# A two-block transformer kernel: the first units of six following stages computed in two token halves

## The chip, the cores and the metric

The kernel runs on one core of one Trainium2 chip. A core has TensorE (matmul, PE), VectorE (DVE), ScalarE (ACT), GpSimd (POOL) and SyncE, which here only issues loads. TensorE multiplies out of SBUF into PSUM, eight banks of 128 partitions x 512 fp32. Each engine runs its own instruction list; semaphores order them. The metric is device time in microseconds (us) of one execution, lower is better.

## The reference

Input x is 1 x 512 tokens x 1024. Two blocks of two layers each follow one another, in fp32:

```python
for i in range(2):                               # first block, post-norm
    mix = sconv_ssd_mixer(x, ...) if i == 0 else fox_mixer(x, ...)
    x = layer_norm(ALPHA * x + mix, ln_mix_g[i], ln_mix_b[i])
    x = layer_norm(ALPHA * x + conv_ffn(x, ...), ln_ffn_g[i], ln_ffn_b[i])
for i in range(2):                               # second block, gated pre-norm
    sh1, sc1, g1, sh2, sc2, g2 = split(silu(c) @ ada_w[i] + ada_b[i])
    h = rmsnorm(x, norm1_g[i]) * (1 + sc1) + sh1
    x = x + g1 * (gqa_attention(h, ...) if i == 0 else chunked_gmlp(h, ...))
    h = rmsnorm(x, norm2_g[i]) * (1 + sc2) + sh2
    x = x + g2 * (square(relu(h @ mlp_w_in[i])) @ mlp_w_out[i])
```

Each stage needs its input whole in the channel direction: the normalisation takes the mean over all 1024 channels of a token, and each product sums over them.

## The kernel before

**Products.** To keep fp32 accuracy at the speed of the one-pass type fp32r, each operand is split into a high part (its fp32r rounding) and a low part (the rest), and each product is three matmuls: high x high, high x low, low x high. Weights come in *units* of 128 x 1024, 444 in all, through a ring of four slots: SyncE loads `raw`, ScalarE copies it to `whi`, GpSimd subtracts to `wlo` (L558). The products of a 1024-channel input take 24 matmuls of 512 columns per unit.

**Stages.** There are stages of two forms. In the "f" form (`pe_f`: up0, fqk, up1, mu0, mu1) a unit gives 128 output channels for all 512 tokens: the weights stand in the array, the activations `xhi`, `xlo` (channel block k of 8 on the partitions, tokens along the columns) stream through. In the "t" form (`pe_t_unit`) tokens stand in the array. The projections back to 1024 channels (out0, dn0, fo, dn1, o, md0, go, md1; `pe_t_jit`) are of the t form in two column halves, with token tile t of four in PSUM bank t (first half) or 4 + t (second half). Their last two units are ordered by tile in `pe_t_tail`, so that tile 0 is complete first and tile 3 last.

**A boundary.** Between a projection and the next stage lie the residual and the norm. `q` numbers it: 1 is out0 to up0, 2 dn0 to fqk, 3 fo to up1, 4 dn1 to qkv, 5 o to mu0, 6 md0 to gv, 7 go to mu1. For each token tile, VectorE adds the residual (`dve_ln_tile`, or `dve_gated_tile` in the second block), takes the moments, ScalarE takes the root, VectorE the reciprocal and writes `nrm`, in column halves of 512 (the first holds channel blocks 0 to 3). TensorE transposes `nrm` in blocks of 128 x 128 into PSUM banks 0 to 3 (L1897): blocks k = 0 to 3 of each tile as it comes (`pe_xt_tile`), k = 4 to 7 later (`pe_xt_late`), since they use the same four banks. ScalarE applies the norm's gain and shift per channel on the way from PSUM to a two-slot buffer `xf` (`act_xt`, L646), VectorE splits `xf` into `xhi` (a cast, L1217) and `xlo` (a subtract, L1219) (`dve_xt`). Then the first three units of the next stage run k by k, nine matmuls for each k, with one late block's transposes between (`pe_f`, L1987 to L1997).

**Fillers.** `pe_busy` issues transposes of the identity into an unused bank (L1902). `KEEP_BUSY = (0, 18, 0, 16)` puts 18 after tile 1's transposes and 16 after tile 3's in `pe_t_tail`.

**Residual pass.** In boundaries 1 to 3 the residual itself is replaced by the norm's output, `xres = nrm * g + b`, in eight whole-tile operations that `dve_resid` places between the splits (L1491, L1495), beginning after k = 3.

**Order.** All of it is written out by hand, engine by engine. ScalarE copies the next stage's third unit during the tail (`act_next_whi(name, 2)`), its fourth after `act_xt`. In boundary 2 it also loads `wf_raw`, the weights of the forget gate (L1136), ahead of `act_xt` and copies it behind (L1139).

## Time and profile before

| | us |
|---|---|
| median of 3 runs | 2811.45 (2811.03 to 2812.35) |
| the profiled execution, whole | 2811.43 |
| its span, first to last instruction | 2809.5 |
| TensorE busy | 2783.7 (99%) |
| VectorE busy | 1303.3 (46%) |
| GpSimd busy | 1140.6 (41%) |
| ScalarE busy | 1081.2 (38%) |

The page gives busy time by engine; a busy TensorE can also be busy with fillers. Matmuls overlap: a duration of 0.39 us is from the first column in to the last result out, while the next one starts 0.23 us after it. The step from start to start is what a matmul costs in a row. The mean granted clock was 0.998 of full speed.

### The profile page before, as it was taken

To read this page: it belongs to the slowest core of one execution; us is meant where nothing else is said; L and a number is where in the kernel's file an instruction comes from. 1 tells how busy PE (TensorE), PEld (TensorE's weight loads), DVE (VectorE), ACT (ScalarE), POOL (GpSimd) and SP (SyncE) were. 2 spreads that over 40 slices of the span, in tenths; PEclk is the share of its full clock that TensorE was granted. 3 is DMA by queue.
4 is the path that set the end of the run, shared out by engine and by line. 5 is a ranking of instruction groups with operands and counts; after the bars stand their busy time and mean duration, and the time that the engine had idled before them with its cause. 6 is when DMAs were issued, how large, how long until landed. Compare 5 with 4: busy or idle time off the path is not lost.

```text
span 2809.5 us, 37915 instructions
## 1 busy us (share of the span) xinstructions
PE 2783.7 (99%) x13890; PEld 2287.7 (81%) x13890; DVE 1303.3 (46%) x1516; ACT 1081.2 (38%) x1574; POOL 1140.6 (41%) x472
## 2 busy tenths in 40 slices
...
GB/s 160 90 69 74 90 103 267 239 140 88 99 88 95 9 76 232 244 169 102 97 73 45 2 74 106 97 105 98 86 135 94 90 78 103 90 92 96 104 98 75
DMA packets 319812, 299.95 MB, mean 107 GB/s; under 512 B 16268, under 2 KB 251224, under 8 KB 319576
## 3 DMA queue, kind: packets, MB, share of 16 engines
...
## 4 chain that ended last, share of the span: by engine, by line
PE 46%; issue 36%; POOL 16%; DVE 1%; ACT 0%; POOLq 0%; DVEq 0%; ACTq 0%
POOL wlo L558 16%; PE ps L2034 8%; PE ps L2035 8%; PE ps L2036 8%; PE ps L1892 6%; PE ps L1894 6%; PE ps L1893 6%; PE ps L2319 1%; PE ps L2255 1%; PE ps L2284 1%; PE ps L2394 1%; PE ps L2065 0%; PE ps L2067 0%; PE ps L2066 0%; PE ps L1897 0%
## 5 line engine op out<-in xcount | busy, mean ns | idle before, releaser
L558 POOL TENSOR_TENSOR wlo<-raw,whi 128x1024 fp32r<-128x1024 f32 x444 | 1115.3, 2515 | 1630.6 <-ACT whi L616 1630.3
L1892 PE MATMUL ps<-xhi,whi 128*128 128x512 f32 x1824 | 718.0, 394 | 0.3
L1894 PE MATMUL ps<-xhi,wlo 128*128 128x512 f32 x1824 | 710.3, 389 | 0.0
L1893 PE MATMUL ps<-xlo,whi 128*128 128x512 f32 x1824 | 709.9, 389 | 0.0
L616 ACT ACTIVATE whi<-raw 128x1024 fp32r<-128x1024 f32 x444 | 466.3, 1052 | 288.9 <-PE ps L2036 167.8
L2034 PE MATMUL ps<-whi,ahi 128*128 128x512 f32 x1184 | 461.4, 390 | 0.7 <-DVE alo L1396 0.7
L2036 PE MATMUL ps<-whi,alo 128*128 128x512 f32 x1184 | 460.7, 389 | 0.0
L2035 PE MATMUL ps<-wlo,ahi 128*128 128x512 f32 x1184 | 460.6, 389 | 0.0
L1892 PEld LDWEIGHTS ps<-xhi,whi 128*128 128x128 f32 x1824 | 342.5, 188 | 73.1 <-issue 3.2
L1894 PEld LDWEIGHTS ps<-xhi,wlo 128*128 128x128 f32 x1824 | 342.3, 188 | 71.7
L1893 PEld LDWEIGHTS ps<-xlo,whi 128*128 128x128 f32 x1824 | 342.6, 188 | 71.0 <-issue 1.4
L2034 PEld LDWEIGHTS ps<-whi,ahi 128*128 128x128 f32 x1184 | 222.2, 188 | 47.6 <-DVE alo L1396 0.8
L2035 PEld LDWEIGHTS ps<-wlo,ahi 128*128 128x128 f32 x1184 | 222.3, 188 | 46.0
L2036 PEld LDWEIGHTS ps<-whi,alo 128*128 128x128 f32 x1184 | 222.2, 188 | 46.0
L1396 DVE TENSOR_TENSOR alo<-hid_mlp,ahi 128x1024 fp32r<-128x1024 f32 x60 | 76.4, 1273 | 242.1 <-ACT ahi L795 242.1
L1739 DVE SCALAR_TENSOR_TENSOR hid_mlp<-ps,relu 128x512 f32 (+1 forms) x64 | 44.3, 692 | 281.4 <-ACT relu L1033 281.4
L2034 PE MATMUL ps<-whi,xhi 128*128 128x512 f32 x416 | 163.1, 392 | 0.9 <-POOL wlo L558 0.7
L2036 PE MATMUL ps<-whi,xlo 128*128 128x512 f32 x416 | 162.0, 389 | 0.0
L2035 PE MATMUL ps<-wlo,xhi 128*128 128x512 f32 x416 | 161.9, 389 | 0.0
L1541 DVE SCALAR_TENSOR_TENSOR acc<-adaraw,ccol,acc 128x1536 f32<-128x1536 f32 x56 | 154.3, 2793 | 2.4 <-DMA adaraw<-in_ada_w 2.1
L795 ACT ACTIVATE ahi<-hid_mlp 128x1024 fp32r (+1 forms) x60 | 63.7, 1062 | 205.2 <-PE ps L2036 205.2
L1033 ACT ACTIVATE relu<-ps 128x512 f32<-128x512 f32 x64 | 38.3, 599 | 229.3 <-PE ps L1894 229.3
...
## 6 DMA issues: line engine op xcount, KB each, us to landing
...
```

What stands on the lines that cost most here:

```text
L558: pool.tensor_tensor(wlo[:, j], raw[:, j], whi[:, j].bitcast(F32), ALU.subtract).then_inc(w_lo, 1)
L616: act.activation(whi[:, s], raw[:, s], ACT.Copy).then_inc(w_hi, 1)
L795: act.activation(ahi[:, (m0 + j) % 2], x, ACT.Copy).then_inc(a_hi, 1)
L1396: dve.tensor_tensor(alo[:, s], x, ahi[:, s].bitcast(F32), ALU.subtract).then_inc(a_lo, 1)
L1541: dve.scalar_tensor_tensor(x, adaraw[s][:], ccol[:, bass.ds(i, 1)], x, ALU.mult, ALU.add).then_inc(ada_acc, 1)
L1739: dve.scalar_tensor_tensor(hid_mlp[:, bass.ds(e, 1)], ps[:, bank_f(j):bank_f(j) + 1], 0.0, relu[:, j % 2:j % 2 + 1], ALU.max, ALU.mult).th ...
L1892: pe.matmul(out, lh, rh, start=start, stop=False)
L1893: pe.matmul(out, lh, rl, start=False, stop=False)
L1894: return pe.matmul(out, ll, rh, start=False, stop=stop)
L2034: pe.matmul(out, lh[:, k, c], wh[:, k], start=st, stop=False, skip_group_check=True)
L2035: pe.matmul(out, lh[:, k, c], wl[:, k], start=False, stop=False, skip_group_check=True)
L2036: ins = pe.matmul(out, ll[:, k, c], wh[:, k], start=False, stop=False, skip_group_check=True)
```

## The change

At the six boundaries 1, 2, 3, 5, 6 and 7 (`PARTED`) the blocks k = 0 to 3 go through in two parts of 256 tokens: part 0 is tiles 0 and 1, part 1 tiles 2 and 3. TensorE transposes part 0 inside the tail of the projection and part 1 among the products of the next stage. ScalarE applies gain and shift to a half block in place in PSUM, VectorE splits it straight from PSUM. The products of k = 0 to 3 of the first three units run for 256 columns at a time in the f form; gv, of the t form, runs its first two units by pairs of tiles. Blocks 4 to 7 go on as before, but all four are transposed in a row after part 1. The fillers at these boundaries go. The residual pass begins ahead of k = 4. Semaphore counts become the tables `XT0` and `EV0`. Two scratch tiles lay in the room of `xhi`'s first blocks: `gate` moves up by 8 KB, and the squares of the RMS norm, of which only the sums are used, are written to `nrm`. In the diff, `product(e, k, c)` is the three matmuls of unit e and block k on columns c. Its core:

```diff
+PARTED = (1, 2, 3, 5, 6, 7)
+PART = (slice(0, 256), slice(256, 512))
...
+    def act_xt_part(act, q, scale, bias, h):
+        c = PART[h]
+        for k in range(4):
+            act.wait_ge(xt_tp, XT0[q] + 4 * h + k + 1)
+            act.activation(ps[:, k, c], ps[:, k, c], ACT.Identity, scale=scale(k), bias=bias(k)).then_inc(xt_ev, 1)
...
     def act_ln_tail(act, r, name, g_ap, b_ap, scale, bias):
         act_next_whi(act, name, 1)
         act_sqrt_table(act, r)
+        act_ln_std(act, r, 0)
+        act_ln_std(act, r, 1)
+        act_xt_part(act, r + 1, scale, bias, 0)
+        act_ln_std(act, r, 2)
+        act_next_whi(act, name, 2)
+        act_ln_std(act, r, 3)
         load_gb(act, gb, g_ap, b_ap)
+        act_xt_part(act, r + 1, scale, bias, 1)
+        act_xt(act, r + 1, scale, bias, 4)
...
@@ act_rms_tail @@
         for t in range(NT):
-            if t == 2 and early:
-                act_next_whi(act, name, 2)
+            if t == 2:
+                if early:
+                    act_next_whi(act, name, 2)
+                act_xt_part(act, r + 1, norm_scale(s), norm_shift(s), 0)
...
+    def dve_xt_part(dve, q, h):
+        c = PART[h]
+        for k in range(4):
+            dve.wait_ge(xt_ev, EV0[q] + 4 * h + k + 1)
+            dve.tensor_copy(xhi[:, k, c], ps[:, k, c]).then_inc(xt_hi, 1)
+            dve.wait_ge(xt_hi, XT0[q] + 4 * h + k + 1)
+            dve.tensor_tensor(xlo[:, k, c], ps[:, k, c], xhi[:, k, c].bitcast(F32), ALU.subtract).then_inc(xt_lo, 1)
...
@@ dve_ln_tail @@
+        for h in range(2):
+            dve_ln_moments(dve, r, name, h and 3)
+            if not h:
+                dve_ln_moments(dve, r, name, 1)
+            for t in (2 * h, 2 * h + 1):
+                dve_ln_inverse(dve, r, t)
+                norm(t, 0)
+            if not h:
+                dve_ln_moments(dve, r, name, 2)
+            dve_xt_part(dve, r + 1, h)
         for t in range(NT):
             norm(t, 1)
+        dve_xt(dve, r + 1, resid=r, k0=4)
...
@@ dve_rms_tail @@
+        tile(0)
+        tile(1)
+        for t in range(2):
+            inverse(t)
+            norm(t, 0)
+        tile(2)
+        dve_xt_part(dve, 5 + s, 0)
+        tile(3)
+        for t in range(2, 4):
+            inverse(t)
+            norm(t, 0)
+        dve_xt_part(dve, 5 + s, 1)
+        for t in range(NT):
             norm(t, 1)
+        dve_xt(dve, 5 + s, k0=4)
...
@@ pe_f @@
-            for k in range(KD):
-                pe.wait_ge(xt_lo, KD * q + k + 1)
-                for e in range(3):
...
-                if k < 4:
-                    pe_xt_late(pe, q, k + 4)
+            def product(e, k, c, stop=False):
...
+            for h in range(2):
+                for k in range(4):
+                    pe.wait_ge(xt_lo, XT0[q] + 4 * h + k + 1)
+                    for e in range(2):
+                        if not h and k == 0:
+                            pe.wait_ge(w_lo, S + e + 1)
+                            pe.wait_ge(res_add, 8 * q - 3 + e)
+                        product(e, k, PART[h])
+                if h:
+                    for k in range(4, KD):
+                        pe_xt_late(pe, q, k)
+                for k in range(4):
+                    if not h and k == 0:
+                        pe.wait_ge(w_lo, S + 3)
+                        pe.wait_ge(res_add, 8 * q - 1)
+                    if not h and k == 3:
+                        pe_xt_part(pe, q, 1)
+                    product(2, k, PART[h])
+            for k in range(4, KD):
+                pe.wait_ge(xt_lo, XT0[q] + 4 + k + 1)
+                for e in range(3):
+                    ins = product(e, k, slice(0, T), k == KD - 1)
...
+            pe.wait_ge(res_add, 8 * q)
...
@@ pe_t_tail @@
-            if q and q != 4 and t == 2 and i:
-                pe_xt_tile(pe, q, 0)
-        if q:
-            for t in range(0 if q == 4 else 1, NT):
+            if q in PARTED and (t, i) == ((2, 1) if q < 4 else (3, 0)):
+                pe_xt_part(pe, q, 0)
+        if q == 4:
+            for t in range(NT):
...
@@ pe_gm @@
+        unit(0, 0, 1, blocks=XT0[6], tiles=(0, 1), done=False)
+        unit(0, 1, 1, blocks=XT0[6] + 2, tiles=(0, 1), done=False, mid=lambda: pe_xt_part(pe, 6, 1))
         pe.wait_ge(res_add, 48)
+        unit(0, 0, 1, blocks=XT0[6] + 4, tiles=(2, 3))
+        for k in range(4, KD):
+            pe_xt_late(pe, 6, k)
+        unit(0, 1, 1, blocks=XT0[6] + 6, tiles=(2, 3))
```

How it moves instructions, at boundary 1, from the projection's tail to the fourth unit of up0. ScalarE before, from the third and fourth root on (`std` is the root, `xf` the affine, `whi` a weight unit):

```order
L616 ACTIVATE whi<-raw 128x1024 [waits unit_done,raw_in2]
L836 ACTIVATE std<-mv,eps_ln 128x1 [waits aggr_done] x2
L831 DMA gb<-in_ln_mix_g 128x1024
L832 DMA gb<-in_ln_mix_b 128x1024
L646 ACTIVATE xf<-ps,tab 128x512 [waits xt_tp] x2
L646 ACTIVATE xf<-ps,tab 128x512 [waits xt_lo,xt_tp] x6
L853 UNCONDITIONAL_BRANCH
L616 ACT_TABLE_LOAD [waits unit_done]
L616 ACTIVATE whi<-raw 128x1024 [waits raw_in3]
```

ScalarE after, from the first two roots on:

```order
L856 ACTIVATE std<-mv,eps_ln 128x1 [waits aggr_done] x2
L657 ACTIVATE ps<-ps,tab 128x256 [waits xt_tp] x4
L856 ACTIVATE std<-mv,eps_ln 128x1 [waits aggr_done]
L622 ACTIVATE whi<-raw 128x1024 [waits unit_done,raw_in2]
L856 ACTIVATE std<-mv,eps_ln 128x1 [waits aggr_done]
L851 DMA gb<-in_ln_mix_g 128x1024
L852 DMA gb<-in_ln_mix_b 128x1024
L657 ACTIVATE ps<-ps,tab 128x256 [waits xt_tp] x4
L666 ACTIVATE xf<-ps,tab 128x512 [waits xt_lo,xt_tp] x4
L877 UNCONDITIONAL_BRANCH
L622 ACT_TABLE_LOAD [waits unit_done]
L622 ACTIVATE whi<-raw 128x1024 [waits raw_in3]
```

Four half affines now stand between the roots of tiles 1 and 2, four behind the loads of gain and shift, and four whole ones are left.

VectorE before, from tile 0's reciprocal to tile 2's norm (`xres` the residual, `stats` and `mv` the moments):

```order
L1441 RECIPROCAL rstd<-std 128x1 [waits std_done]
L1448 TENSOR_SCALAR nrm<-xres,mv,rstd 128x512 [waits rstd_done]
L1420 SCALAR_TENSOR_TENSOR xres<-xres,ps 128x512 [waits tile_done]
L1422 BN_STATS stats<-xres 128x6 [waits res_add]
L1436 BN_AGGR mv<-stats 128x2 [waits stat_done]
L1441 RECIPROCAL rstd<-std 128x1 [waits std_done]
L1448 TENSOR_SCALAR nrm<-xres,mv,rstd 128x512 [waits rstd_done]
L1448 TENSOR_SCALAR nrm<-xres,mv,rstd 128x512
```

VectorE after, from tile 0's reciprocal to the first half split:

```order
L1479 RECIPROCAL rstd<-std 128x1 [waits std_done]
L1486 TENSOR_SCALAR nrm<-xres,mv,rstd 128x512 [waits rstd_done]
L1479 RECIPROCAL rstd<-std 128x1 [waits std_done]
L1486 TENSOR_SCALAR nrm<-xres,mv,rstd 128x512 [waits rstd_done]
L1458 SCALAR_TENSOR_TENSOR xres<-xres,ps 128x512 [waits tile_done]
L1460 BN_STATS stats<-xres 128x6 [waits res_add]
L1474 BN_AGGR mv<-stats 128x2 [waits stat_done]
L1244 CAST xhi<-ps 128x256 [waits xt_ev]
L1246 TENSOR_TENSOR xlo<-ps,xhi 128x256 [waits xt_hi]
```

Tile 1's reciprocal and norm moved ahead of tile 2's residual, the second-half norm of tile 0 is gone from here, and the splits of part 0 follow tile 2's moments.

VectorE after, from the last half split of part 1 to k = 6:

```order
L1244 CAST xhi<-ps 128x256 [waits xt_ev]
L1246 TENSOR_TENSOR xlo<-ps,xhi 128x256 [waits xt_hi]
L1486 TENSOR_SCALAR nrm<-xres,mv,rstd 128x512 x4
L1531 TENSOR_TENSOR xres<-nrm,gb 128x1024 [waits nrm_done,gb_in]
L1531 TENSOR_TENSOR xres<-nrm,gb 128x1024
L1255 CAST xhi<-xf 128x512 [waits xt_ev]
L1257 TENSOR_TENSOR xlo<-xf,xhi 128x512 [waits xt_hi]
L1535 TENSOR_TENSOR xres<-xres,gb 128x1024 [waits res_mul]
L1255 CAST xhi<-xf 128x512 [waits xt_ev]
L1257 TENSOR_TENSOR xlo<-xf,xhi 128x512 [waits xt_hi]
L1531 TENSOR_TENSOR xres<-nrm,gb 128x1024
L1255 CAST xhi<-xf 128x512 [waits xt_ev]
```

The four second-half norms and the first two operations of the residual pass stand ahead of the split of k = 4.

ScalarE at boundary 2 before, from the loads to the fourth unit of fqk:

```order
L831 DMA gb<-in_ln_ffn_g 128x1024
L832 DMA gb<-in_ln_ffn_b 128x1024
L1136 DMA wf_raw<-in_fox_w_in 128x8x16
L646 ACTIVATE xf<-ps,tab 128x512 [waits xt_tp] x2
L646 ACTIVATE xf<-ps,tab 128x512 [waits xt_lo,xt_tp] x6
L1139 ACTIVATE wf_hi_t<-wf_raw 128x128 [waits small_in]
L616 ACTIVATE whi<-raw 128x1024 [waits unit_done,raw_in1]
```

And after:

```order
L851 DMA gb<-in_ln_ffn_g 128x1024
L852 DMA gb<-in_ln_ffn_b 128x1024
L657 ACTIVATE ps<-ps,tab 128x256 [waits xt_tp] x4
L666 ACTIVATE xf<-ps,tab 128x512 [waits xt_lo,xt_tp] x4
L1163 DMA wf_raw<-in_fox_w_in 128x8x16
L1165 ACTIVATE wf_hi_t<-wf_raw 128x128 [waits small_in]
L622 ACTIVATE whi<-raw 128x1024 [waits unit_done,raw_in1]
```

The load of `wf_raw` moved from before the affines to right before the copy that waits for it.

## Rows read from the trace of the kernel before

**Rows 1.** The page, busy us, share of the span and instructions of each engine.

```profile
PE 2783.7 (99%) x13890; PEld 2287.7 (81%) x13890; DVE 1303.3 (46%) x1516; ACT 1081.2 (38%) x1574; POOL 1140.6 (41%) x472
```

**Rows 2.** TensorE's groups: line, operation, shapes, count; busy us, mean ns; idle before.

```profile
L1902 PE MATMUL ps<-consts 128*128 128x128 f32 x276 | 36.8, 293 | 2.8 <-DMA consts<-in_consts 2.8
```

**Rows 3.** TensorE's timeline, out0 to up0: start, duration, operation; idle and its releaser.

```profile
390.07 0.40 PE L2066 MATMUL ps<-wlo,ahi 128*128 128x512 f32 x1
...
392.35 0.40 PE L2067 MATMUL ps<-whi,alo 128*128 128x512 f32 x1
...
393.02 2.13 PE L1902 MATMUL ps<-consts 128*128 128x128 f32 x18
...
396.47 1.91 PE L1902 MATMUL ps<-consts 128*128 128x128 f32 x16
398.45 0.47 PE L1892 MATMUL ps<-xhi,whi 128*128 128x512 f32 x1
...
408.52 0.48 PE L1892 MATMUL ps<-xhi,whi 128*128 128x512 f32 x1
```

**Rows 4.** TensorE's timeline in the first attention: scores of width 256.

```profile
939.32 0.28 PE L2300 MATMUL ps<-klo,qhi 64*128 64x256 f32 x2
939.44 0.28 PE L2300 MATMUL ps<-khi,qlo 64*128 64x256 f32 x2
```

**Rows 5.** VectorE's groups by shape: splits, and operations of 256 columns from PSUM.

```profile
L1217 DVE CAST xhi<-xf 128x512 fp32r<-128x512 f32 x56 | 23.6, 422 | 21.1 <-ACT xf L646 21.0
...
L1219 DVE TENSOR_TENSOR xlo<-xf,xhi 128x512 fp32r<-128x512 f32 x56 | 38.8, 692 | 1.9
...
L1210 DVE CAST xhi<-ps 128x512 fp32r<-128x512 f32 x8 | 5.5, 683 | 10.2 <-PE ps L1897 10.2
...
L1315 DVE COPY b_tok<-ps 128x256 f32<-128x256 f32 x2 | 0.8, 422 | 0.0
...
L1339 DVE TENSOR_TENSOR cbm<-ps,consts 128x256 f32<-128x256 f32 x4 | 1.7, 422 | 4.8 <-PE ps L2186 4.8
```

**Rows 6.** ScalarE's groups: the affine of 512 columns, and one column.

```profile
L646 ACT ACTIVATE xf<-ps,modc,nscale 128x512 f32<-128x512 f32 x32 | 24.3, 778 | 30.4 <-PE ps L1897 25.0 <-DVE xlo L1219 5.4
...
L836 ACT ACTIVATE std<-mv,eps_ln 128x1 f32<-128x1 f32 x16 | 4.7, 291 | 21.5 <-DVE mv L1436 21.4
```

**Rows 7.** VectorE's timeline at the same boundary, tile 0's norm and tile 2's residual.

```profile
388.68 0.55 DVE L1448 TENSOR_SCALAR nrm<-xres,mv,rstd 128x512 f32<-128x512 f32 x1
389.53 0.69 DVE L1420 SCALAR_TENSOR_TENSOR xres<-xres,ps 128x512 f32<-128x512 f32 x1 [0.31 <-PE ps L2067]
```

**Rows 8.** Timeline of ScalarE, VectorE and GpSimd at the end of that boundary.

```profile
409.60 1.28 ACT L616 ACT_TABLE_LOAD   x1
...
410.89 1.06 ACT L616 ACTIVATE whi<-raw 128x1024 fp32r<-128x1024 f32 x1
...
411.39 1.22 DVE L1491 TENSOR_TENSOR xres<-nrm,gb 128x1024 f32<-128x1024 f32 x1
...
412.04 2.82 POOL L558 TENSOR_TENSOR wlo<-raw,whi 128x1024 fp32r<-128x1024 f32 x1 [17.06 <-ACT whi L616]
...
412.52 3.42 DVE L1495 TENSOR_TENSOR xres<-xres,gb 128x1024 f32<-128x1024 f32 x1
```

**Rows 9.** VectorE's timeline, go to mu1: tile 3's gate multiply and its norm.

```profile
2448.94 0.70 DVE L1631 TENSOR_TENSOR ps<-ps,gate 128x512 f32<-128x512 f32 x1 [0.80 <-PE ps L2067]
...
2451.68 0.49 DVE L1650 TENSOR_SCALAR nrm<-xres,rstd 128x512 f32<-128x512 f32 x1
```

**Rows 10.** The tile wf_raw: its two loads, from issue to landing.

```profile
DMA to landing us min/median/max: 4.1/5.4/6.8
```

**Rows 11.** Stretches at out0-up0 and dn1-qkv: length, busy us by engine, granted clock.

```profile
392.50:398.40 5.90, 5.70 (x48) 4.91 (x45) 5.44 (x13) 1.96 (x5) 2.37 (x1) 1.00 0.42 143
1415.30:1418.10 2.80, 0.17 (x1) 0.00 (x0) 2.69 (x5) 1.65 (x4) 0.00 (x0) 1.00 0.00 0
1421.70:1431.70 10.00, 6.88 (x31) 6.47 (x32) 4.92 (x8) 7.31 (x14) 0.00 (x0) 0.50 0.00 0
```

More of the change, by code:

```diff
@@ L82 @@
 GU_SLOTS = 4
+PARTED = (1, 2, 3, 5, 6, 7)
+XT0 = [0]
+for _q in range(8):
+    XT0.append(XT0[-1] + (12 if _q in PARTED else 8))
+EV0 = [_n - 8 for _n in XT0]
+PART = (slice(0, 256), slice(256, 512))
 NRM_ORDER = ((0, 0), (1, 0), (0, 1), (2, 0), (3, 0), (1, 1), (2, 1), (3, 1))
@@ L232, in build_in @@
     gb = actmem("gb", [P, 2, D], 0)
-    gate = scratch("gate", [P, D], 0)
+    gate = scratch("gate", [P, D], 8)
     junk = scratch("junk", [P, D], 4)
@@ L1653, in dve_rms_tail, with tile @@
         dve.tensor_scalar(mv[:, :, 1], sumsq[:, :, 0], 1.0 / D, EPS, ALU.mult, ALU.add).then_inc(half_sq, 1)
-        for t in range(NT):
+        def tile(t):
             wait_tile(dve, 4 + s, name, t)
             dve_gated_tile(dve, s, 1, t)
-            if t:
-                inverse(t - 1)
-                norm(t - 1, 0)
-            if t == 2:
-                norm(0, 1)
-        inverse(3)
-        norm(3, 0)
-        for t in range(1, NT):
+        tile(0)
[11 more added lines that the diff above has]
+        for t in range(NT):
             norm(t, 1)
+        dve_xt(dve, 5 + s, k0=4)
     def dve_last_tail(dve, s, name):
@@ L1923, in pe_xt_tile, with pe_xt_part @@
                 ins.then_inc(xt_tp, 1)
+    def pe_xt_part(pe, q, h):
+        if h == 0:
+            pe.wait_ge(res_add, 8 * q - 4)
+        pe.wait_ge(nrm_done, 8 * (q - 1) + 2 * h + 2)
+        for k in range(4):
+            if h:
+                pe.wait_ge(xt_lo, XT0[q] + k + 1)
+            for t in (2 * h, 2 * h + 1):
+                ins = pe_xt_block(pe, nrm, k, t)
+            ins.then_inc(xt_tp, 1)
     def pe_xt_late(pe, q, k):
         pe.wait_ge(nrm_done, 8 * q)
-        pe.wait_ge(xt_ev, KD * (q - 1) + k - 3)
+        if q in PARTED:
+            pe.wait_ge(xt_lo, XT0[q] + k + 1)
+        else:
+            pe.wait_ge(xt_ev, EV0[q] + k - 3)
         for t in range(NT):
@@ L1948, in pe_table, with pe_f @@
                 ins.then_inc(tab_tp, 1)
-    def pe_f(pe, name, freed, q=None, first=(), after=None):
+    def pe_f(pe, name, freed, q=None, after=None):
         S, n = U0[name], NUNITS[name]
@@ L1963, in unit @@
             ins.then_inc(unit_done, 1)
-        for s, v in first:
-            pe.wait_ge(s, v)
         if q == 0:
@@ L1985, in pe_f @@
         elif q is not None:
-            for k in range(KD):
-                pe.wait_ge(xt_lo, KD * q + k + 1)
+            def product(e, k, c, stop=False):
+                wh, wl = parts(e)
+                out, rh, rl = ps[:, bank_f(e), c], xhi[:, k, c], xlo[:, k, c]
+                pe.matmul(out, wh[:, k], rh, start=k == 0 and c is PART[0], stop=False, skip_group_check=True)
+                pe.matmul(out, wh[:, k], rl, start=False, stop=False, skip_group_check=True)
+                return pe.matmul(out, wl[:, k], rh, start=False, stop=stop, skip_group_check=True)
+            for h in range(2):
[6 more added lines that the diff above has]
+                        product(e, k, PART[h])
+                if h:
+                    for k in range(4, KD):
+                        pe_xt_late(pe, q, k)
+                for k in range(4):
+                    if not h and k == 0:
[6 more added lines that the diff above has]
+                pe.wait_ge(xt_lo, XT0[q] + 4 + k + 1)
                 for e in range(3):
-                    if k == 0:
-                        pe.wait_ge(w_lo, S + e + 1)
-                    wh, wl = parts(e)
-                    ins = mm3(pe, ps[:, bank_f(e)], wh[:, k], wl[:, k], xhi[:, k], xlo[:, k], k == 0, k == KD - 1)
+                    ins = product(e, k, slice(0, T), k == KD - 1)
                     if k == KD - 1:
                         ins.then_inc(unit_done, 1)
-                if k < 4:
-                    pe_xt_late(pe, q, k + 4)
+            pe.wait_ge(res_add, 8 * q)
         for e in range(0 if q is None else 3, RING):
@@ L2019, in pe_f, with pe_t_unit @@
                     unit(i * RING + j, j)
-    def pe_t_unit(pe, start, e, j, bank0, lh, ll, first, blocks=None):
+    def pe_t_unit(pe, start, e, j, bank0, lh, ll, first, blocks=None, tiles=range(NT), done=True, mid=None):
         slot = (start + j) % RING
@@ L2027, in pe_t_unit @@
         for k in range(2):
+            if mid and k:
+                mid()
             if blocks is not None:
                 pe.wait_ge(xt_lo, blocks + k + 1)
-            for t in range(NT):
+            for t in tiles:
                 out = ps[:, bank0 + t]
@@ L2036, in pe_t_unit @@
                 ins = pe.matmul(out, ll[:, k, c], wh[:, k], start=False, stop=False, skip_group_check=True)
-        ins.then_inc(unit_done, 1)
+        if done:
+            ins.then_inc(unit_done, 1)
     def pe_fv(pe):
```

105 lines of the change are left out of this document (47 added, 58 removed).

## The prediction

> **What bounds the kernel now.** I read the page's busy shares first, then TensorE's groups by line, then the timelines of the boundaries, then the groups of VectorE and ScalarE. TensorE is busy in 99% of the span [rows 1], so a change can win only what TensorE does there without use, and loses whatever it newly waits. 276 of its matmuls are fillers (L1902), which multiply the identity and are thrown away [rows 2]; 38 stand at the start, 34 at each of the seven boundaries. The boundary out0 to up0 shows what they cover: the last product of the stage starts at 392.35, the first of the next at 398.45 [rows 3]. Of these 6.10 us, 0.23 is the product itself (ten starts from 390.07 to 392.35) and 1.31 are 12 useful transposes at 0.109 (18 fillers in 2.13, which is 17 steps and one full duration of 0.28). So 4.57 us is lost per boundary: 3.71 in fillers, the rest in short waits. The other boundaries have the same form. Six of the seven are changed: 27 us is all there is to win.
>
> **What TensorE does in place of it.** Per boundary the first three units of k 0 to 3 become 72 products of 256 columns in place of 36 of 512 (not in gv, whose products keep their width). The width 256 in this data type is seen in the attention scores, in pairs on two row halves: 939.32 to 939.44 is 0.118 a pair [rows 4]. From below it is half of 0.227, 0.113; from above the 0.227 itself would be the end, if a product had a floor there. I take 0.118, the nearest row: 72 x 0.118 - 36 x 0.227 = +0.33 us. By the Trainium skill, "TensorE: Matmul & The Clock Gate", Back-to-back issue gap, a warm product takes N/2.4 + 2.5 ns, 109 ns here and 0.3 us less than nothing per boundary; the same rule gives 216 for 512 columns where the trace has 227, so the trace decides.
>
> **The halves on VectorE and ScalarE.** A split of 512 columns from SBUF is a cast of 0.422 and a subtract of 0.692. From PSUM a cast of 512 takes 0.683 (the subtract does not change), and operations of 256 columns from PSUM take 0.422 each [rows 5]. A half block thus costs 0.42 + 0.03 + 0.42 - 0.08 = 0.79 us (gaps and overlaps of this size stand between neighbours, as 411.39 + 1.22 and 412.52 in [rows 8]), two halves 1.58 where the whole from SBUF is 1.06. Bounds: 0.58 if the cast kept its SBUF speed (0.21), 1.32 if a half cost what a whole from PSUM does. ScalarE's affine is 0.778 for 512 columns, its one-column operation 0.291 [rows 6], so 256 columns come to about 0.54; it is written back to PSUM, which no row shows (0.3 to 0.8).
>
> **The schedule of a LayerNorm boundary (up0; fqk and up1 alike).** All times from the rows of this boundary.
> - Part 0 needs the normalised half of tile 1. Before, norm of tile 0 started at 388.68 for 0.55 and tile 2's residual at 389.53 [rows 7]. Now the reciprocal and norm of tile 1 stand ahead of it: done at 389.84. TensorE, which had its four transposes at 389.37, waits to 389.98: 0.64 lost. Eight transposes and tile 3's 12 products then end at 393.65.
> - VectorE does tile 2's moments (1.66) to 391.41 and four half splits to 394.57, the first ready at 392.2. TensorE's 24 products of units 0 and 1 (0.71 per k) run behind them from 393.65 without a wait worth naming, then unit 2 to 397.55. The weights of unit 2 are ready at about 396.1, 1.1 later than before, still in time.
> - VectorE: tile 3's moments to 396.15, norms of tiles 2 and 3 to 397.38. Part 1's transposes start at 397.55, no wait. They and three products end at 398.81. But transpose, affine 0.54 and split 0.84 take 1.9 us: the first half block is ready at 399.45. Wait 0.7, and 0.24 more since VectorE's 0.79 per k is slower than TensorE's 0.71. Done at 402.57.
> - The second column halves are now normalised only after part 1: four norms at a step of 0.46 from 401.72, to 403.63. The late transposes wait 1.2.
> - Then VectorE does both scales of the residual (2.35) before k=4, since that call moved ahead of the loop: its split is ready at 406.97, where TensorE arrives. k=5 is ready at 409.17, k=6 at 411.37, 2.2 us a step against TensorE's 2.04: another 0.4 lost.
> Sum of waits 0.64 + 0.94 + 1.2 + 0.4 = 3.2. Against 4.57, with 0.33 for the width, the boundary gains 1.0 us: k=7 ends at 415.7 instead of 408.52 + 4 x 2.04 = 416.7 [rows 3].
>
> **The port at up0 and up1.** A VectorE add of two SBUF operands that starts while GpSimd splits weights takes 3.42 instead of 1.22, and ends after GpSimd's 2.82 [rows 8]. Before, the last affine waited for TensorE's last transposes, so table load (409.60), weight copy (410.89) and GpSimd's start (412.04) fell behind the last split, and hit only the residual pass. Now that affine waits only for the split of k=5; call its end T (409.17). ScalarE: 0.09 + 0.78 + 1.28 + 1.06 and gaps, GpSimd starts at T + 3.33. VectorE: scale 1.14, split of k=6 1.06, shift 1.14: the cast of k=7 starts at T + 3.25, its subtract at T + 3.70. GpSimd comes between and the subtract waits it out: k=7 is ready at T + 6.6, not T + 4.4. TensorE loses 2.2 us at each of the two. By the Trainium skill, "SBUF — State Buffer", Who interferes with whom, whoever starts first holds the shared ports for its whole instruction; by that rule a start 0.4 later would save it all. Net -1.2 each.
>
> **The load of the forget weights at fqk.** ScalarE used to issue the wf_raw load before its affines and copy it after them. Now all affines lie ahead of the load and the copy comes right behind it, with the weights of unit 3 queued after. Loads of this tile landed 4.1 and 6.8 us after issue [rows 10], the longer one behind two gain rows on its queue. Issued at T + 0.2, it lands at T + 4.2; copy 0.3, weights 1.06, GpSimd 2.4 (perhaps after a shift of VectorE): T + 7.9 to T + 9.0. TensorE needs unit 3 at T + 6.5: 1.3 to 2.5 lost (4 with 6.8). I take 1.9, net -0.9.
>
> **The gated boundaries (mu0, mu1, gv).** No residual pass there. In mu0 and mu1 ScalarE copies a weight unit (1.05) ahead of part 0's affines. On the clock of go to mu1, TensorE is through tile 3 at 2449.2 (four transposes later than before), the first split comes at 2449.55, the fourth three steps of 0.79 later at 2451.9. Only then VectorE takes tile 3: from gate multiply to the end of its norm 3.2, as 2448.94 to 2452.17 [rows 9], so 2455.0. TensorE ends its 33 half products at 2453.7: part 1 waits 1.4. The rest as in the LayerNorm case: 0.4 for part 0, then 0.7, 0.25, 1.0 for the late transposes, 0.2 in small ones, 4.0 in all. 4.6 - 0.33 - 4.0 gives +0.3 each. In gv the two parts hide better (waits 1.1 and 1.0), but the third unit's weights are copied after the last affine as before, and bind: +0.6.
>
> **Sum.** -1.2 - 0.9 - 1.2 + 0.3 + 0.3 + 0.6 = -2.1 of gain. The profiled execution took 2811.43 us around its span of 2809.5, and the median is 2811.45, so one sum serves both: 2811.4 + 2.1 = 2813.5 us. The 22 us of removed fillers (204 x 0.109) come back as waits for VectorE, which worked beside the fillers.
>
> **The rivals.** Less than 0.2% (5.6 us) is not told from no change.
> - A: the forecast, 2809 to 2818. Chance 0.47.
> - B: GpSimd starts after the subtract of k=7, and the wf_raw load is hidden. It needs 0.4 us at T and a landing of 2 us. For it speaks that the port is missed by so little. The boundaries gain 3 x 1.0 + 1.2: 2807.2. With half splits of 0.7 the four steps of part 1 keep up with TensorE, and it becomes some 2804. Chance 0.23, half of it beyond 0.2%.
> - C: the halves overlap so well that nearly all fillers' time is won: 6 x 4.2 = 25 us, 2786. For it speaks that TensorE gets 2.7 us of tile 3 to cover part 0; against it that VectorE is filled in part 1. Chance 0.09.
> - D, slower: half operations cost what whole ones from PSUM do, 1.32 a split. Then each part is VectorE's: 4 x 0.53 = 2.1 us in part 1, about 1 in part 0, 18 over six boundaries: 2831. It decides from about 0.95 us a split (6 us). For it: PSUM to PSUM is unseen. Against: 422 in both 256-column rows. With the long landing of wf_raw, chance 0.14.
> - E: the fillers kept the clock up. At dn1 to qkv TensorE was 0.17 busy in 2.80 us and the clock fell to 0.50 [rows 11]; the 13.6 us at that level, 6.88 of 10 busy, cost 3.5 to 7. My longest wait is 1.4 us between products, so 0.07: 2820 for one boundary. By the Trainium skill, "TensorE: Matmul & The Clock Gate", Part 4: PE-mode transpose, transposes don't count as work for the clock; by that rule the fillers never held it, and 392.5 to 398.4, transposes alone, does stand at 1.00 [rows 11].
> Faster: C, half of B and a little of A's tail, 0.22. Slower: most of D and E and A's tail, 0.22. Same 0.56. The range is 2804 to 2821; A's own is 2809 to 2818.
>
> **What would show it.** In the profile after: L1902 down to 72; waits of TensorE on VectorE's nrm about 13 us in all and on xlo about 11; half casts and subtracts of 0.42 each, affines near 0.54; the last subtract of up0 and up1 at about 3 us with GpSimd beside it; wf_hi_t waiting for its DMA some 4 us, and unit 3 of fqk for wlo. Wrong would be: full-speed subtracts there, a 256-column step of 0.15 or more, a clock below 1.00 at a changed boundary, or first products of the next stage later than 0.1 us after tile 3 in up0.

## The result, and the profile after

The changed kernel took 2818.95 us (median of 7 runs, 2817.11 to 2822.62) against 2811.45 of the kernel before: ratio 1.0028, 95% interval 1.0018 to 1.0038. It is slower by 7.5 us, 5.4 more than forecast. That is inside the whole range of 2804 to 2821, but outside the 2809 to 2818 of A, the forecast itself. By more than 0.2% it is "slower", which was given 0.22. The profiled execution took 2820.08 us, one of the slower of the seven. Its span is 2818.1, so it carries 8.6 us of difference to the span of 2809.5.

The page's busy row, beside [rows 1]:

```profile
PE 2769.0 (98%) x13866; PEld 2275.8 (81%) x13866; DVE 1320.2 (47%) x1564; ACT 1085.6 (39%) x1598; POOL 1139.3 (40%) x472
```

TensorE's busy time fell by 14.7 us, yet the span grew: where fillers were there is now idle time, and more of it. The groups of after by shape, for [rows 2], [rows 5] and [rows 6]:

```profile
L1945 PE MATMUL ps<-consts 128*128 128x128 f32 x72 | 11.2, 324 | 2.9 <-DMA consts<-in_consts 2.9
...
L1244 DVE CAST xhi<-ps 128x256 fp32r<-128x256 f32 x48 | 19.8, 413 | 8.6 <-ACT ps L657 8.6
...
L1246 DVE TENSOR_TENSOR xlo<-ps,xhi 128x256 fp32r<-128x256 f32 x48 | 20.4, 424 | 1.6
...
L1257 DVE TENSOR_TENSOR xlo<-xf,xhi 128x512 fp32r<-128x512 f32 x32 | 26.2, 820 | 1.1
...
L657 ACT ACTIVATE ps<-ps,tab 128x256 f32<-128x256 f32 x24 | 11.4, 535 | 9.4 <-PE ps L1940 9.4
```

The fillers are down to 72, and the half operations cost what was estimated: 413 and 424 ns, the affine to PSUM 535. The whole-block subtract has a mean of 820 instead of 692: some of the 32 were held up. What TensorE waited for: the total in us, how often, and the longest:

```profile
PE ps L1940 <- DVE nrm L1690: 5.0, 6, 1.1
PE ps L1935 <- DVE wf_lo_t L1873: 4.3, 1, 4.3
PE ps L2046 <- DVE xlo L1257: 4.2, 3, 1.9
PE ps L1940 <- DVE nrm L1486: 4.2, 6, 0.9
PE ps L2046 <- DVE xlo L1246: 3.3, 7, 0.5
```

Four of these five were forecast. The second, the wait for `wf_lo_t` (the low part of the forget gate's weights), was not. To see where the time lies, the span is cut at the first product of each projection's tile-wise tail (before: 381.10, 754.75, 1030.63, 1404.27, 1650.01, 2007.53, 2437.30, 2794.51; after: 380.88, 755.80, 1037.57, 1414.43, 1660.49, 2017.46, 2446.48, 2803.15). Each cell is the length of the stretch minus that of the kernel before, in us; a run's e-number is that of the next section:

| stretch with | forecast | after | e1 | e2 | e3 | e4 | e7 | e5 | e9 | e6 | e8 | e10 |
|---|---|---|---|---|---|---|---|---|---|---|---|---|
| start | 0 | -0.2 | -0.4 | -0.5 | -0.2 | 0.4 | 0.6 | -0.1 | -0.4 | 0.0 | -0.2 | 1.3 |
| up0 | 1.2 | 1.3 | 0.0 | 3.0 | 4.1 | 1.4 | 1.4 | 1.3 | 1.3 | 1.3 | -0.7 | 1.4 |
| fqk | 0.9 | 5.9 | 0.0 | 1.9 | 7.9 | 4.4 | 7.0 | -0.3 | -0.2 | -1.1 | -2.6 | 1.5 |
| up1 | 1.2 | 3.2 | 0.0 | 1.5 | 4.2 | 1.5 | 1.5 | 1.3 | 1.5 | 1.7 | -0.7 | 2.8 |
| q4, unchanged | 0 | 0.3 | -0.5 | -0.3 | 0.6 | 0.2 | 0.1 | 0.7 | -0.4 | 0.7 | -0.1 | -0.5 |
| mu0 | -0.3 | -0.5 | -0.6 | -0.6 | -0.1 | 0.8 | -0.5 | -0.5 | -0.5 | -0.5 | -0.5 | 2.2 |
| gv | -0.6 | -0.7 | -0.8 | -0.8 | -0.8 | -0.8 | -0.7 | -0.8 | -0.7 | -0.7 | -0.7 | 2.1 |
| mu1 | -0.3 | -0.5 | -0.5 | -0.5 | -0.5 | 0.8 | -0.5 | -0.5 | -0.5 | -0.5 | -0.5 | 2.8 |

Of the 3.0 of e2 and the 4.1 of e3 in up0, some 1.7 is a stretch at half clock. In q4 the kernels at 0.1 or more have such a stretch of 3.41 us in the second attention (after at 1521.3), the others have none.

The forecast of up0 holds in its parts. The timelines of VectorE and GpSimd there (for [rows 8]) and of TensorE (for [rows 3]), start, duration, operation, idle before:

```profile
412.91 2.73 DVE L1257 TENSOR_TENSOR xlo<-xf,xhi 128x512 fp32r<-128x512 f32 x1
```
```profile
412.54 2.56 POOL L564 TENSOR_TENSOR wlo<-raw,whi 128x1024 fp32r<-128x1024 f32 x1 [16.64 <-ACT whi L622]
```
```profile
413.40 0.39 PE L2048 MATMUL ps<-xhi,wlo 128*128 128x512 f32 x1
415.70 0.50 PE L2046 MATMUL ps<-xhi,whi 128*128 128x512 f32 x1 [1.91 <-DVE xlo L1257]
```

GpSimd starts 0.37 us ahead of the subtract of k=7, which takes 2.73; TensorE's step from 413.40 to 415.70 is 2.30 where 0.227 is normal, 2.07 lost (forecast 2.2). The waits ahead of it in that boundary lose 0.71, 0.70, 1.02 and 0.30 (forecast 0.64, 0.94, 1.2, 0.4).

fqk is another matter. VectorE there, then GpSimd, then TensorE:

```profile
787.94 0.69 DVE L1257 TENSOR_TENSOR xlo<-xf,xhi 128x512 fp32r<-128x512 f32 x1
788.55 3.42 DVE L1531 TENSOR_TENSOR xres<-nrm,gb 128x1024 f32<-128x1024 f32 x1
791.89 6.74 DVE L1535 TENSOR_TENSOR xres<-xres,gb 128x1024 f32<-128x1024 f32 x2
798.56 2.42 DVE L1873 TENSOR_TENSOR wf_lo_t<-wf_raw,wf_hi_t 128x128 fp32r<-128x128 f32 x1
```
```profile
788.00 2.89 POOL L564 TENSOR_TENSOR wlo<-raw,whi 128x1024 fp32r<-128x1024 f32 x1 [17.07 <-ACT whi L622]
791.31 9.52 POOL L564 TENSOR_TENSOR wlo<-raw,whi 128x1024 fp32r<-128x1024 f32 x3 [0.43 <-ACT whi L622]
```
```profile
796.37 0.39 PE L1937 MATMUL ps<-xhi,wlo 128*128 128x512 f32 x1
801.04 0.60 PE L1935 MATMUL ps<-xhi,wf_hi_t 128*16 128x512 f32 x1 [4.28 <-DVE wf_lo_t L1873]
801.44 0.63 PE L1936 MATMUL ps<-xlo,wf_hi_t 128*16 128x512 f32 x1
```

The subtract of k=7 started 0.06 us before GpSimd and ran at full speed. Then four VectorE instructions in a row each met a GpSimd split: 3.42 us, the two of 6.74 together, and 2.42, instead of three times 1.22 and once 0.28. The last is wf_lo_t, and TensorE waits 4.28 us for it. The two loads of the tile wf_raw, for [rows 10] (the shorter time is the one at fqk), and two stretches (length, busy us by engine, granted clock, DMA share, GB/s):

```profile
DMA to landing us min/median/max: 2.3/3.2/4.1
```
```profile
801.10:804.50 3.40, 3.40 (x9) 1.14 (x10) 2.83 (x6) 0.00 (x0) 0.00 (x0) 0.50 0.55 154
1074.20:1077.50 3.30, 3.30 (x9) 2.61 (x8) 3.26 (x5) 3.13 (x4) 1.76 (x1) 0.50 0.99 327
```

The load landed after 2.3 us, not 4. And the clock stands at 0.50 (1.2 of 2.4 GHz) right behind the wait in fqk, and again in up1, 1.5 us behind the wait of 1.91 for k=7's subtract; each of these lasts 3.41 us. TensorE issues products in a row in both, at a step of 0.427 us where 0.23 is normal, so each costs 1.6 to 1.7 us. In up0 the same wait left the clock at 1.00.

### The profile page after: what moved, and what is told of

The parts are those of the page before. It is cut to its first block, busy times and chain, and to the rows that moved or that the text cites. A ratio compares the mean times of both kernels' runs of the same rounds, so it can differ in the third digit from the quotient of the medians.

```text
span 2818.1 us, 37950 instructions
## 1 busy us (share of the span) xinstructions
PE 2769.0 (98%) x13866; PEld 2275.8 (81%) x13866; DVE 1320.2 (47%) x1564; ACT 1085.6 (39%) x1598; POOL 1139.3 (40%) x472
## 4 chain that ended last, share of the span: by engine, by line
issue 48%; PE 28%; POOL 21%; DVE 1%; POOLq 0%; ACT 0%; DVEq 0%; ACTq 0%
POOL wlo L564 20%; PE ps L2113 5%; PE ps L2115 5%; PE ps L2114 5%; PE ps L1935 3%; PE ps L1936 3%; PE ps L1937 3%; PE ps L2474 1%; PE ps L2145 0%; PE ps L2147 0%; PE ps L2146 0%; POOLq L563 0%; POOL rb L590 0%; POOL ra L587 0%; POOL qr L593 0%
## 5 line engine op out<-in xcount | busy, mean ns | idle before, releaser
L1935 PE MATMUL ps<-xhi,whi 128*128 128x512 f32 x1704 | 669.5, 393 | 1.8 <-POOL wlo L564 1.7
L1936 PE MATMUL ps<-xlo,whi 128*128 128x512 f32 x1704 | 663.6, 389 | 0.0
L1937 PE MATMUL ps<-xhi,wlo 128*128 128x512 f32 x1704 | 663.5, 389 | 0.0
L1935 PEld LDWEIGHTS ps<-xhi,whi 128*128 128x128 f32 x1704 | 320.2, 188 | 70.7 <-issue 2.2
L1937 PEld LDWEIGHTS ps<-xhi,wlo 128*128 128x128 f32 x1704 | 320.1, 188 | 67.1
L1936 PEld LDWEIGHTS ps<-xlo,whi 128*128 128x128 f32 x1704 | 320.3, 188 | 66.5 <-issue 1.4
```

Source lines behind the costliest of these rows:

```text
L1935: pe.matmul(out, lh, rh, start=start, stop=False)
L1936: pe.matmul(out, lh, rl, start=False, stop=False)
L1937: return pe.matmul(out, ll, rh, start=False, stop=stop)
```

## The experiments

Times are medians, with the ratio to the kernel before, run again beside them (2810.82, 2811.23 or 2811.37 us), and its 95% interval. The table shows the profiled execution of each.

**e1, the three gated boundaries alone.** `PARTED = (5, 6, 7)`, and the functions of the LayerNorm boundaries as they were.

> Only the three gated boundaries (o to mu0, md0 to gv, go to mu1) are changed; the three after LayerNorm are put back word for word, their 34 transposes of the identity each included. Theory (the loss lies wholly after the LayerNorms): out0, dn0 and fo cost what they cost in the kernel before, and the gated ones keep what the trace of after shows for them, -0.55, -0.75 and -0.54 us, so the span is about 1.8 us shorter than the kernel before, some 2809.6 us, and against the kernel before the time is the same within what can be measured. Rival (halves are bad in themselves and the gated stages only look better because they start later): the gated stages gain nothing or lose here, 2811 to 2813 us.

2809.66 us, 0.9995 (0.9986 to 1.0004); in the table the LayerNorm stretches are back at 0.0 and the gated ones keep their -0.5 to -0.8. So the loss lies wholly behind the LayerNorms, and halves are no burden in themselves at the gated boundaries.

**e2, the forget weights split early.**

```diff
             dve.tensor_tensor(xlo[:, k], xf[:, k % 2], xhi[:, k].bitcast(F32), ALU.subtract).then_inc(xt_lo, 1)
+            if resid == 1 and k == KD - 1:
+                dve.wait_ge(wf_hi, 2)
+                dve.tensor_tensor(wf_lo_t[:], wf_raw[:], wf_hi_t[:].bitcast(F32), ALU.subtract).then_inc(wf_lo, 1)
             if resid is not None:
                 dve_resid(dve, resid, k)
```

> The changed kernel with one part of the fqk boundary moved: wf_raw is loaded right after the gamma and beta loads, its high part is made between the affines of k=5 and k=6, and the low part wf_lo_t stands right behind the subtract of k=7, ahead of the last three instructions of the residual pass. Theory (wf_lo_t is late because the residual pass ahead of it is locked out by GpSimd time after time, and TensorE's 4.3-us wait then halves the clock for 3.4 us): wf_lo_t ends near 789, the wait of 4.3 us on it and the stretch at 0.5 in fqk go, and the time is 5 to 6 us below the changed kernel, 2813 to 2814 us. Rival (late next: VectorE's residual pass still ends near 799, and the first fqk outputs that VectorE must take out of PSUM are late by the same): TensorE waits 3 to 4 us a unit later on fqk_lo, the time stays at 2818 to 2819. Rival 2 (the halves themselves cost it): nothing goes, 2819.

2818.13 us, 1.0025 (1.0016 to 1.0035), its profiled execution, the fastest of its ten, at 2815.24. The wait on wf_lo_t is gone and fqk costs 1.9 instead of 5.9. But another one came. VectorE, then GpSimd:

```profile
787.96 3.42 DVE L1547 TENSOR_TENSOR xres<-xres,gb 128x1024 f32<-128x1024 f32 x1
791.30 0.41 DVE L1264 CAST xhi<-xf 128x512 fp32r<-128x512 f32 x1
```
```profile
787.74 2.56 POOL L564 TENSOR_TENSOR wlo<-raw,whi 128x1024 fp32r<-128x1024 f32 x1 [15.31 <-ACT whi L622]
```

With nothing to wait for, ScalarE delivers unit 3 sooner, GpSimd starts sooner, and the residual shift ahead of k=7's cast is locked out: TensorE waits 2.1 us for k=7. In the profiled execution a stretch at 0.50 stood in up0 this time (416.6 us) and none in fqk or up1. The theory holds for the wait and neither rival does, but the time moved by only 0.8 us of the 5 to 6 expected, which is not told from nothing.

**e3, the residual pass wholly behind k=7** (`for k in range(3, KD): dve_resid(dve, resid, k)` after the loop).

> The changed kernel with the residual pass (8 instructions of VectorE a boundary) moved wholly behind the subtract of k=7 at the three LayerNorm boundaries, instead of being spread over the splits of k=4 to 7. Theory (the last subtract is late because each k of 4 to 7 carries a 1.2-us residual instruction, and in up0 and up1 it then meets GpSimd's split and takes 2.7 us): the subtract of k=7 ends 4 us earlier and meets no GpSimd instruction, the wait of 1.9 us ahead of k=7's products in up0 and in up1 goes, with the stretch at 0.5 in up1, so about 4 to 5.5 us are gained there; fqk gains 0.5 to 2 in its products, but its wf_lo_t is still behind the pass and as late or later, so TensorE's wait there stays or grows by up to 2. Sum 2814 to 2817 us. Rival (late next: eight residual instructions in a row, each locked out by a GpSimd split, hold VectorE's first instructions of the feed-forward back until after TensorE needs the bank): waits on ff_dve of 2 to 6 us in up0 and up1, and 2819 to 2826 us.

2826.57 us, 1.0056 (1.0042 to 1.0069). The rival won, 0.6 us beyond its range. `gt` is the first result that VectorE takes out of PSUM in the feed-forward, and TensorE waits for its bank. TensorE's waits in up0, and VectorE there:

```profile
PE ps L1934 <- DVE gt L1568: 3.9, 1, 3.9
```
```profile
411.56 3.42 DVE L1534 TENSOR_TENSOR xres<-xres,gb 128x1024 f32<-128x1024 f32 x1
414.90 1.21 DVE L1530 TENSOR_TENSOR xres<-nrm,gb 128x1024 f32<-128x1024 f32 x1
416.04 3.42 DVE L1534 TENSOR_TENSOR xres<-xres,gb 128x1024 f32<-128x1024 f32 x1
```

The wait for k=7 went, and 3.9 us for the first feed-forward results took its place (7.8 in up0 and up1 together); in fqk the wait for wf_lo_t grew to 6.9.

**e4 and e7, fillers in the waits.** e4 puts 12 ahead of k=7 and 32 ahead of the forget gate's products:

```diff
+                if k == KD - 1 and q != 2:
+                    for _ in range(12):
+                        pe.transpose(ps[:, 0, 0:P], ident, ident)
                 pe.wait_ge(xt_lo, XT0[q] + 4 + k + 1)
```

> The changed kernel with transposes of the identity put into two waits of TensorE and nothing else: 12 (1.3 us) ahead of the products of k=7 in up0 and up1, where it waits 1.9 us, and 32 (3.5 us) ahead of the forget gate's products in fqk, where it waits 4.3 to 4.6 us. Theory (the two stretches of 3.41 us at half the clock, in fqk and up1, are made by these waits, and each costs 1.7 us on top of the wait): both stretches are gone, the waits end when they ended, and the time is about 3.4 us below the changed kernel, 2815 to 2816 us. Rival (the clock falls for another reason, or the work in these stretches waits for other engines anyway): the stretches stay or go without the time moving, 2818 to 2819 us.

2820.29 us, 1.0035 (1.0021 to 1.0048), not the 2815 to 2816 of its theory. The condition also took in mu0 and mu1, which its expectation did not say: there the fillers cost 1.3 and 1.4 us. Where they stand in a wait they did what the theory says: both stretches at 0.50 are gone, up1 falls from 3.2 to 1.5 and fqk from 5.9 to 4.4, 3.2 us together. up1 in e4, at 1.00 where after has 0.50:

```profile
1074.00:1078.00 4.00, 4.00 (x19) 3.33 (x18) 3.92 (x5) 3.97 (x5) 2.52 (x1) 1.00 0.88 289
```

e7 is e4 with `q in (1, 3)`.

> The fillers of e4 without those that also stood ahead of the products of k=7 in mu0 and mu1, where TensorE hardly waits and where 12 of them cost 1.4 us each: here only in up0, up1 and ahead of the forget gate's products. Theory of the clock (two stretches of half clock of 3.4 us, in fqk and one of up0 and up1, cost 1.7 us each): the time is 2.7 us below e4 and about 1.5 to 3 us below the changed kernel, 2816 to 2817.5 us. Rival (what the fillers save there is lost to a stretch elsewhere): 2818.5 to 2820 us.

2818.30 us, 1.0025 (1.0016 to 1.0034): between theory and rival, 2.0 below e4, and not told from the changed kernel. So the medians of e4 and e7 do not show what the clock costs; the stretches in the traces do. In e7's profiled execution (2820.32, the slowest of its eleven) mu0 and mu1 are back, but fqk is 7.0. VectorE and GpSimd there:

```profile
789.05 2.89 DVE L1257 TENSOR_TENSOR xlo<-xf,xhi 128x512 fp32r<-128x512 f32 x1
```
```profile
789.03 2.36 POOL L564 TENSOR_TENSOR wlo<-raw,whi 128x1024 fp32r<-128x1024 f32 x1 [17.13 <-ACT whi L622]
```

GpSimd was first, by 0.02 us. The subtract waited, TensorE with it (2.1 us, and a stretch at 0.50), while wf_lo_t was on time (done at 795.55, needed at 801.2), so the 32 fillers stood in no wait and cost 3.4 us. In e4, whose instructions in fqk are the same, VectorE was first by 0.01 us, and wf_lo_t was late again (2.44 us from 799.30):

```profile
788.66 0.69 DVE L1257 TENSOR_TENSOR xlo<-xf,xhi 128x512 fp32r<-128x512 f32 x1
```
```profile
788.67 2.94 POOL L564 TENSOR_TENSOR wlo<-raw,whi 128x1024 fp32r<-128x1024 f32 x1 [17.02 <-ACT whi L622]
```

The same program order thus has two outcomes in fqk, and the traces differ by hundredths of a microsecond ahead of them.

**e5 and e9, fewer residual instructions ahead of k=7.** e5 is e2 with this:

```diff
-        if k == 5:
-            scale(2)
-        if k == 6:
-            shift(1)
         if k == KD - 1:
+            scale(2)
+            shift(1)
             scale(3)
```

> e2 (the forget weights split early) with two instructions of the residual pass, scale of tile 2 and shift of tile 1, moved from behind the splits of k=5 and k=6 to behind that of k=7. In e2 the subtract of k=7 took 2.7 us beside GpSimd in up0 and up1, and in fqk the shift ahead of k=7's cast took 3.42 us beside it, and TensorE waited 1.9, 1.9 and 2.1 us. Theory (the port is the cause, and the splits of k=6 and k=7 can be over before GpSimd starts): these three waits go, k=7's subtract takes 0.7 us in all three, and the five residual instructions behind it end no later than in the changed kernel. LayerNorm stages then cost, against the kernel before, about -0.7, 0 and -0.5 us, and the time is 2806 to 2809 us. Rival (late next, as where all eight instructions stood behind): gt is late by 1 to 4 us in up0 and up1, and the time is 2811 to 2817 us.

2812.55 us, 1.0004 (0.9995 to 1.0013), between theory and rival. All three waits for k=7 went, 5.6 us under e2, but gt is 1.3 us late in up0 and in up1. e9 puts scale(2) back behind k=5 in up0 and up1.

> e5 with the scale of tile 2 back behind the split of k=5 in up0 and up1 (fqk as in e5): of the residual pass only the shift of tile 1 has moved behind k=7 there. Theory (each residual instruction behind k=7 is paid in gt's lateness, and one place fewer is enough, because the table load of 1.28 us ahead of ScalarE's split holds GpSimd back in up0 and up1): k=7's subtract still takes 0.7 us, the waits of 1.3 us on gt go, and the time is 1.5 to 2.6 us below e5, 2810 to 2811 us. Rival (k=7's subtract meets GpSimd again): it takes 2.7 us, TensorE waits 1.5 to 2 us there, 2812 to 2816 us.

2812.30 us, 1.0002 (0.9993 to 1.0012). The expectation was wrong: k=7's subtract takes 0.69, but gt is as late as in e5. VectorE, and TensorE's wait:

```profile
411.74 0.69 DVE L1266 TENSOR_TENSOR xlo<-xf,xhi 128x512 fp32r<-128x512 f32 x1
412.35 1.22 DVE L1547 TENSOR_TENSOR xres<-xres,gb 128x1024 f32<-128x1024 f32 x1
413.48 3.43 DVE L1543 TENSOR_TENSOR xres<-nrm,gb 128x1024 f32<-128x1024 f32 x1
416.83 4.55 DVE L1547 TENSOR_TENSOR xres<-xres,gb 128x1024 f32<-128x1024 f32 x2
```
```profile
PE ps L1946 <- DVE gt L1582: 1.3, 1, 1.3
```

Two GpSimd splits (from 412.49 and 416.54) each hold one residual instruction, whether five stand behind k=7 (e5) or four (e9). In the changed kernel the first hold fell on k=7's subtract and the three behind ran at 1.21: its cost was moved, not saved.

**e6 and e8, VectorE's own chain.** e6 is e5 with the four second-half norms on ScalarE:

```diff
+        act.wait_ge(nmr_done, 2 * r + h + 1)
+        for t in (2 * h, 2 * h + 1):
+            act.activation(nrm[:, t, HALF:], xres[:, t, HALF:], ACT.Identity, scale=rstd[:, t:t + 1],
+                           bias=nmr[:, t:t + 1]).then_inc(nrm_b, 1)
```

> e5 with the four second-half norms of a LayerNorm boundary (0.54 us each) taken off VectorE: ScalarE makes them as an affine with the reciprocal as scale and minus mean times reciprocal as bias, two behind the first part's affines and two behind the second part's; VectorE makes that bias for two tiles at a time, one small instruction each. Theory (what is left of the bubble is VectorE's own chain, and here 4 x 0.455 us less 2 x 0.15 us leave it): the wait of 0.9 to 1.2 us ahead of the late transposes and the one of 0.4 us ahead of the last products of the half go at each of the three boundaries, about 1.3 us each, and the time is 3 to 4 us below e5, 2803 to 2805 us. Rival (the same waits are then set by ScalarE, whose two norms of the second part stand behind four affines and take 0.6 us each): the late transposes wait as long as before, and the time is that of e5 within 1 us.

2811.97 us, 1.0001 (0.9992 to 1.0010), no gain clear of the noise: the rival's time, but not by the rival's reason. VectorE in up0 of e6, and of e8 below it:

```profile
404.03 2.36 DVE L1555 TENSOR_TENSOR xres<-nrm,gb 128x1024 f32<-128x1024 f32 x2 [2.13 <-DMA gb<-in_ln_mix_b]
406.31 0.42 DVE L1276 CAST xhi<-xf 128x512 fp32r<-128x512 f32 x1
```
```profile
401.63 2.35 DVE L1556 TENSOR_TENSOR xres<-nrm,gb 128x1024 f32<-128x1024 f32 x2
404.04 0.43 DVE L1277 CAST xhi<-xf 128x512 fp32r<-128x512 f32 x1
```

The norms' 2 us became a wait for gamma and beta, with k=4's split queued behind it. e8 issues these loads at the end of the tail, with the order of e9:

```diff
         act_next_whi(act, name, 2)
+        act.wait_ge(unit_done, END[name])
+        load_gb(act, gb, g_ap, b_ap)
         act_norm_b(act, r, 0)
         act_ln_std(act, r, 3)
-        load_gb(act, gb, g_ap, b_ap)
```

> e6 with two edits: gamma and beta are loaded right behind the second whi of the tail, 3 us earlier (the first instruction of the residual pass waited until 404.0 us in e6 for them, and the split of k=4 stood behind it, ready since 404.2 us but begun at 406.3), and in up0 and up1 the scale of tile 2 is back behind the split of k=5, so that four and not five residual instructions stand behind k=7. Theory (e6 gained nothing because the loads took the place of the norms, and the 1.3-us waits on gt in up0 and up1 come from the fifth instruction): the wait of 1.4 to 1.7 us ahead of k=4's products goes at all three boundaries and the one on gt at two; the LayerNorm stages then cost -1.4, -2.5 and -1 us against the kernel before, and the time is 2804 to 2807 us, below both kernels and below the gated edit alone (2809.66). Rival (VectorE's first feed-forward instruction is late because GpSimd locks out whatever stands there): waits on gt stay at 1 us or more, 2808 to 2810 us.

2805.51 us, 0.9981 (0.9972 to 0.9990): 0.2% faster than the kernel before, and every LayerNorm stretch now gains, 0.7, 2.6 and 0.7 us. The waits of 1.3 on gt stayed, as its rival said; the gain came without them.

**e10, the kernel before without its fillers** (`pe_busy` stays only after dn1).

> The kernel before without the 34 transposes of the identity at each of its five LayerNorm and gated boundaries of this kind (the 16 and 18 after dn1 stay): TensorE waits in their place, 3 to 4 us in two pieces. Theory (they fill a wait and the waits alone are too short or too broken up to lower the clock): the time stays within 1 us of the kernel before. Rival (a wait of 2 us or more lowers the clock for 3.41 us, as it did in up1 of the changed kernel, in fqk and up0 of others): stretches at 0.5 appear at one to four of the boundaries, at 1.7 us each, 2813 to 2818 us.

2824.24 us, 1.0048 (1.0033 to 1.0062). The rival, and more: all six boundaries have a stretch at 0.50, two of 3.41 us and four of 6.83. TensorE's waits of e10 in up0, then a window in up1 of e10 and of the kernel before:

```profile
PE ps L1897 <- DVE nrm L1448: 2.2, 1, 2.2
PE ps L1892 <- issue: 1.8, 1, 1.8
```
```profile
1051.50:1058.20 6.70, 5.99 (x16) 4.86 (x17) 6.08 (x10) 2.38 (x4) 0.00 (x0) 0.50 0.44 142
```
```profile
1051.50:1058.20 6.70, 6.70 (x37) 5.57 (x36) 6.60 (x10) 1.61 (x3) 0.00 (x0) 1.00 0.01 2
```

16 products in 6.70 us against 37. From the last product of a projection to the first of the next stage it takes 6.07 to 6.34 us in e10 and 6.10 to 6.19 before: the waits stand where the fillers stood, and no gap grew by more than 0.15 us. So what the fillers were worth is the clock: 12.8 us over the six boundaries, where the six stretches make 34 us at half speed. (The expectation says five boundaries; there are six.)

## Why the prediction held, and where it was short

The time came out inside the range, and in part by luck. Above the 2818 of A, the range reaches only as far as rival E (one fall of the clock, 2820, chance 0.07). The clock did fall, but the largest single term, 4.4 us for wf_lo_t, stood in no rival. One of the prediction's own signs of being wrong came true: a clock below 1.00 at a changed boundary. The other three did not.

- **Widths and half operations**: right. 413 + 424 ns and 535 for the affine; a step of 0.120 at width 256 (393.46 to 397.29, 32 steps) where 0.118 was taken.
- **The waits of a LayerNorm boundary**: right, 2.7 measured in up0 against 3.2, and the same in fqk and up1 but for 0.6 in place of the last 0.3 in up1. The view of waits shows 9.2 us on nrm and 7.5 on xlo where 13 and 11 were named. In part the waits were shorter than forecast; in part the view counts from the modelled end of a product, 0.16 us behind its step, and leaves small ones out.
- **The port at up0 and up1**: right in mechanism and size, 2.07 of 2.2. The stretch up0 came out at 1.3 (1.2 forecast). e5, where k=7's subtract meets no GpSimd split, has no wait there, so the collision made it. Moving it gains nothing in up0 (1.3 in after, e5 and e9): it falls on the residual pass and gt.
- **The load of the forget weights**: the step that failed. Forecast: a landing of 4 us, unit 3 late by 1.9. Measured: 2.3 us, and the step into unit 3 lengthened by 0.18. The half-sentence "copy 0.3, weights 1.06, GpSimd 2.4" followed only the weights. It left out the other reader of the load, wf_lo_t, which stands at the end of the residual pass on VectorE, and it stopped counting GpSimd's port at k=7, where it goes on with three more splits. That is 4.4 us of wait and 1.7 of clock. In e2 the wait is gone with wf_lo_t moved forward, and in e4 the stretch at half clock.
- **The clock (rival E)**: given 0.07, with one boundary. It came at two, for 1.7 us each, behind waits of 1.9 and 4.3 us; the prediction named "my longest wait is 1.4", though its own port term is 2.2. The step of 0.427 us shows the price, e10 what the fillers had held. By the Trainium skill, "TensorE: Matmul & The Clock Gate", Part 4: PE-mode transpose, cited beside this rival, transposes don't count as work for the clock. The traces don't agree: with these transposes the clock stayed at 1.00 at all six boundaries, without them it fell at every one.
- **The gated boundaries**: right in sign, -0.5, -0.7 and -0.5 against -0.3, -0.6 and -0.3, and e1 has them alone. The waits of mu0 are those of the forecast: 0.45, 1.22, 0.69 and 0.77 where 0.4, 1.4, 0.95 and 1.0 were named. In gv the third unit's weights do bind, by 1.5 us.
- **Rivals**: B is refuted in up0 and up1 by the 2.73-us subtract. In fqk both its conditions came true (GpSimd 0.06 us behind the subtract, a landing of 2.3 us), and that boundary was the slowest of all, since B too forgot wf_lo_t. C is refuted by the sum of waits, D by 413 and 424 ns.

The sum by these rows: 2.1 forecast, +4.4 for wf_lo_t, +1.7 and +1.7 for the clock, -1.7 for unit 3, -0.6 for the gated stretches. That is 7.6 of the 8.6 us of the profiled executions; the last us lies in fqk (0.6), in up1 and q4 (0.3 each), less 0.2 at the start, and is not taken apart. The medians differ by 7.5. From run to run the changed kernel varies by 5.5 us, the kernel before by 1.4. The two outcomes of fqk and the clock falling at one boundary or another are seen in the profiled executions of different kernels; that they make this spread is an inference, since only one execution of the changed kernel has a trace.
